# Four different orders over the token columns, one for each pair of weight ring slots

## The reference

```python
for i in range(DEPTH):                                   # DEPTH = 2
    h = layer_norm(ALPHA * h + 0.5 * swiglu_ffn(h, ffn_w_in[i, 0], ffn_w_out[i, 0]), ...)
    mix = short_conv_mixer(h, ...) if i % 2 == 0 else gla_mixer(h, ...)
    h = layer_norm(ALPHA * h + mix, ...)
    h = layer_norm(ALPHA * h + 0.5 * swiglu_ffn(h, ffn_w_in[i, 1], ffn_w_out[i, 1]), ...)
return h[:, N_META:]

def swiglu_ffn(h, w_in, w_out):
    gate, up = jnp.split(h @ w_in, 2, axis=-1)
    return (jax.nn.silu(gate) * up) @ w_out
```

## Time and profile before

| | |
|---|---|
| median of 2 runs | 1005.82 us (1005.6 to 1006.03) |
| profiled execution, its own time | 1004.9 us |
| span from its first to its last instruction | 1003.2 us |
| mean granted TensorE clock | 0.998 of full speed |
| matmuls | 7932 |
| busy: TensorE, VectorE, ScalarE, GpSimd | 990.9, 720.5, 511.1, 121.4 us |

### The profile page before, as it was taken

The page is one execution under the profiler, slowest core; times in us unless marked ns, Lnnn a source line. Parts: engine busy times, 40 slices in busy tenths (PEclk is TensorE's granted clock), DMA queues, the critical chain, the costliest instruction groups (busy, mean ns, idle before and its releaser), DMA issues.

```text
span 1003.2 us, 19130 instructions
## 1 busy us (share of the span) xinstructions
PE 990.9 (99%) x7932; PEld 975.0 (97%) x7932; DVE 720.5 (72%) x1077; ACT 511.1 (51%) x743; POOL 121.4 (12%) x136
## 2 busy tenths in 40 slices
PE   9999999999999999999999999999989999999997
PEld 7999999999999999999999999999989999999986
DVE  5866657689899865667697655667897998866543
ACT  6644345465456534344564434445867766544340
POOL 2000002320002000003220000134152320000000
PEclk9999999999999999999999999999999999999999
DMA  9976656637862865556638665565355738966531
GB/s 257 256 205 175 180 163 182 187 94 208 236 178 83 248 194 171 177 170 178 190 99 258 179 180 167 164 177 148 85 148 153 205 106 238 257 194 194 188 130 42
DMA packets 324264, 176.60 MB, mean 176 GB/s; under 512 B 6658, under 2 KB 320048, under 8 KB 324176
## 3 DMA queue, kind: packets, MB, share of 16 engines
q1 hardware_dynamic: 323664, 174.15, 60.0%
q0 software_dynamic: 480, 1.15, 0.4%
q10 hardware_dynamic: 32, 0.07, 0.0%
HBM read 174.29 MB, written 1.05 MB: 175 GB/s over the span
## 4 chain that ended last, share of the span: by engine, by line
PE 92%; DVE 4%; ACT 1%; issue 1%; POOL 1%; POOLq 0%; DVEq 0%; ACTq 0%
PE bank L1316 23%; PE bank L1321 23%; PE bank L1319 23%; PE bank L1335 3%; PE bank L1336 3%; PE bank L1337 3%; PE bank L1476 2%; PE bank L1477 2%; PE bank L1475 2%; PE bank L1360 2%; PE bank L1361 2%; PE bank L1362 2%; DVE weights_lo L824 1%; DVE rms L1224 1%; DVE gate_area L1231 0%
## 5 line engine op out<-in xcount | busy, mean ns | idle before, releaser
L465 ACT ACTIVATE weights_hi<-raw_weights 128x1024 fp32r<-128x1024 f32 x335 | 354.0, 1059 | 401.0 <-PE bank L1321 291.2
L824 DVE TENSOR_TENSOR weights_lo<-raw_weights,weights_hi 128x1024 fp32r<-128x1024 f32 x334 | 415.1, 1249 | 195.3 <-ACT weights_hi L465 194.1
L1316 PE MATMUL bank<-x_hi,weights_hi 128*128 128x272 f32 (+1 forms) x1584 | 224.1, 283 | 0.0
L1321 PE MATMUL bank<-x_lo,weights_hi 128*128 128x272 f32 (+1 forms) x1584 | 222.3, 282 | 0.0
L1319 PE MATMUL bank<-x_hi,weights_lo 128*128 128x272 f32 (+1 forms) x1584 | 222.2, 282 | 0.0
L1316 PEld LDWEIGHTS bank<-x_hi,weights_hi 128*128 128x128 f32 x1584 | 204.0, 188 | 0.7 <-ACT qT L689 0.2
L1321 PEld LDWEIGHTS bank<-x_lo,weights_hi 128*128 128x128 f32 x1584 | 203.7, 188 | 0.0
L1319 PEld LDWEIGHTS bank<-x_hi,weights_lo 128*128 128x128 f32 x1584 | 203.7, 188 | 0.0
L1321 PE MATMUL bank<-mid_lo,weights_hi 128*128 128x272 f32 x462 | 67.0, 285 | 0.0
L1316 PE MATMUL bank<-mid_hi,weights_hi 128*128 128x272 f32 x462 | 66.9, 284 | 0.0
L1319 PE MATMUL bank<-mid_hi,weights_lo 128*128 128x272 f32 x462 | 66.9, 284 | 0.0
(11 more groups left out here) (230 smaller groups left out, 1209.0 us busy)
## 6 DMA issues: line engine op xcount, KB each, us to landing
raw_weights<-in_ffn_w_in_dram SPq DMA_DIRECT2D x176, 512.0 KB, 4.7
raw_weights<-in_ffn_w_out_dram SPq DMA_DIRECT2D x70, 512.0 KB, 3.6
raw_weights<-in_conv_w_in_dram SPq DMA_DIRECT2D x24, 512.0 KB, 4.0
raw_weights<-in_gla_w_in_dram SPq DMA_DIRECT2D x24, 512.0 KB, 3.9
raw_weights<-in_ffn_w_out_dram SPq DMA_DIRECT2D x24, 384.0 KB, 3.1
raw_weights<-in_conv_w_out_dram SPq DMA_DIRECT2D x8, 512.0 KB, 4.7
raw_weights<-in_gla_w_out_dram SPq DMA_DIRECT2D x8, 512.0 KB, 4.9
x_tok<-in_x_dram SPq DMA_DIRECT2D x2, 512.0 KB, 5.0
```

Of the source, the lines that this page charges most:

```text
L465: nc.scalar.activation(w_hi[:, n % RING, :], raw[:, n % RAW, :], ACT.Copy).then_inc(hi_split, 1)
L824: nc.vector.tensor_tensor(w_lo[:, s, :], raw[:, n % RAW, :], w_hi[:, s, :].bitcast(F32), ALU.subtract).then_inc(lo_split, 1)
L1316: nc.tensor.matmul(into, block_of(w_hi, n, k - k0), walk(hi[:, k, cols]), start=first and k == k0, stop=False)
L1321: mm = nc.tensor.matmul(into, block_of(w_hi, n, k - k0), walk(lo[:, k, cols]), start=False, stop=last and k == k1 - 1)
```

## The change

`multiply` no longer has one walk for long tiles (272 columns) and one for short ones (256). It picks the walk by the pair of ring slots in which the unit lies (`n % RING // 2`, 0 to 3):

| slot pair | long tiles | short tiles |
|---|---|---|
| 0 | runs of 4, 4 passes (as before) | runs of 4, 4 passes |
| 1 | runs of 8, 2 passes | runs of 8, 2 passes |
| 2 | runs of 2, 8 passes | runs of 2, 8 passes |
| 3 | runs of 2, 4 passes | one run (as before) |

A run is a stretch of neighbouring words; with `run` words and `passes` passes the step from one run to the next within a pass is run x passes words: 16 in the first three rows, 8 in the fourth. The numbers multiplied and summed are the same.

```diff
--- before.py
+++ after.py
@@ -1302,13 +1302,17 @@
             def block_of(w, n, k):
                 return w[:, n % RING, k * P:(k + 1) * P]
 
-            def by_rows(ap):
-                return ap.rearrange("p (i j e) -> p j i e", e=4, j=4)
+            def in_runs(run, passes):
+                return lambda ap: ap.rearrange("p (i j e) -> p j i e", e=run, j=passes)
+
+            by_rows = in_runs(4, 4)
+            LONG_WALKS = (by_rows, in_runs(8, 2), in_runs(2, 8), in_runs(2, 4))
+            SHORT_WALKS = (by_rows, in_runs(8, 2), in_runs(2, 8), lambda ap: ap)
 
             def multiply(ps, n, source, cols, k0=0, k1=KU, first=True, last=True, ready=None, before_last=None, middles=()):
 
                 hi, lo = source
-                walk = by_rows if ps.shape[-1] == T else lambda ap: ap
+                walk = (LONG_WALKS if ps.shape[-1] == T else SHORT_WALKS)[n % RING // 2]
                 into = walk(ps)
                 if ready is None and before_last is None and not middles:
                     pe.wait_ge(hi_split, n + 1)
```

## The result

The median after the change is 1356.53 us (1356.5 to 1356.57, 2 runs), against 1005.82 us before. The ratio is 1.348 with a 95% interval of 1.346 to 1.351. The prediction was 1021 us, 990 to 1068: the direction was that of its likeliest case, and the size lies far outside its range. The span grew from 1003.2 to 1354.8 us, by 351.6.

What follows compares the result with a forecast made beforehand. TensorE's matmul queue was taken as the bound, count times start-to-start pace. 2.1 + 9.2 + 3.9 = +15.2 us on the profiled 1004.9 gave 1020.1, 1021 us against the median; range 990 to 1068 us.

Steps and rivals of the forecast that it cites:

- likeliest case: Whole kernel: the prediction's own forecast of 1021 us, slightly slower, range 1011 to 1033 us, chance 0.43.
- The frame: Whole kernel: time is the number of TensorE matmuls times the start-to-start pace; 4020 long and 1104 short matmuls change.
- Parts 1 and 3: Runs of 8 in 1404 long matmuls, +2.1 us; all short tiles of `multiply`, together +3.9 us, ends 0 and +8.
- Part 2: Runs of 2 in 2616 long matmuls on pairs 2 and 3: 126 ns each, +9.2 us; ends -6.5 and +47.6 us.
- the item for runs of 2 in part 3: Runs of 2 in 360 short matmuls: slower contiguous pace, +4.5 ns each, 1.6 us.
- Rival C: 2616 long and 360 short matmuls: runs of 2 leave the weight load no spare access; up to 1068 us; chance 0.22.
- R: Theory formed after the profile, not predicted: moving operand read in aligned groups of 4 words, each costing 4 columns' time.
- Rival A: Changed tiles: run length doesn't matter, stalls come from weight loads; about 1008 us, 1003 to 1011; chance 0.24 including D.
- Rivals B and D: B: 4020 long matmuls at 120.0 ns, 996 us, chance 0.11. D: hardware order fixed, 1006 us, within Rival A's 0.24.
- the one on 4 and 8 passes of runs of 2: Long tiles of pairs 3 and 2: their two walks might differ in pace; no size given.

Runs made afterwards that it cites:

- run 11: Kernel before, with runs of 4 also for first_multiply, shift matmuls and y tiles, and multiply_raw's copy rows 276 words apart, not 274: 1008.94 us against 1005.61, ratio 1.003.
- run 7: Kernel before, with the weights of blocks 0 to 6 starting 0, 4, 8 or 2 words later on slot pairs 0 to 3: 1012.55 us.
- run 9: Kernel after with all runs of 2 undone (long tiles back to runs of 4, short to one run): 1011.29 us against 1005.61, ratio 1.005.
- runs 1 to 4: Kernel after: new orders only for the read (1353.63 us), only for the bank write (1027.65), reads 2 words earlier (1124.32), runs of 6, 10 and 12 (1077.05).
- run 2: Kernel after, with the moving operand read in contiguous order and only the PSUM bank written in the four new orders: 1027.65 us.
- runs 5 and 6: Short tiles in one run, long tiles with a different step on each slot pair: all in runs of 4 (1023.68 us), all in runs of 2 (1654.33 us).
- run 8: As run 7, but in blocks 0 to 3 the weights take every second word (pairs 1 and 3) or every fourth (pair 2): 1116.4 us.
- run 3: Kernel after, most long matmuls cut to 256 columns: runs of 4 aligned, read 2 words earlier, or bank 2 words later; one run read 2 earlier: 1124.32 us.
- run 10: Most long matmuls cut to 256 columns, all pairs in runs of 4, moving operand starting 0, 4, 8 or 12 words in: 969.49 us.

## Why the prediction was wrong, step by step

**The frame held.** That the time is a count times a pace, that no wait, DMA or other engine comes in, and the counts for each slot pair: all as read. Three small readings were off and cost nothing. TensorE's longest wait before was 2.0 us, at the very start, and not 1.5. Its idle time fell by 3.9 us (12.3 to 8.4, span less busy) where "unchanged within 1 us" was forecast. And between the two stretches of y tiles in the earlier trace rows lie several shift matmuls, of which the first two, at unit 262, come right before the pace goes from 113 to 117.9 ns. That the pace depends on what went before was a guess from this; run 11 bears it out, run 7 has a case without it.

**Parts 1 and 3 but for runs of 2 held.** Runs of 8 in long tiles: +1.5 ns forecast, +2.3 measured, 3.2 us for 2.1. Short tiles in runs of 4: +0.6 us forecast, 0.0 measured, by luck: +0.9 ns on the 240 of f3, -3.8 ns on the 48 that read y. In runs of 8: 0.9 and 1.1. One run behind another walk: 0.8 and 0.9, at a median of 117 ns, by the kind of carry-over that was read from the earlier trace rows; behind runs of 8 and one run (run 9) the same tiles of f3 stayed at 113.3, so it seems to hang on which walk goes before.

**Part 2 is the step that failed**, and the item for runs of 2 in part 3 with it: 9.2 and 1.6 us were forecast, 307.3 and 37.0 came. The step took the cost of a shorter run for stalls on top of full speed, 126 ns a matmul and 140.7 at most. The runs showed a read that goes by whole 16-byte groups, so that a run of 2 pays for 4 columns: 234.0 and 247.0 ns. The high end of part 2 was "the stalls of the worst row (13.7 ns) twice over". That put a factor of two on the 13.7 ns above full speed, when nothing in the rows excluded that a factor falls on the 113.3 ns of full speed itself. No row of before has a run under 4 words, so the trace gave no bound above, and the one that I set was a guess in the form of a computation. A bound from "half as many words for each access" would have been 2 x 113.3 + 13.7 = 240.4 ns a matmul, 117.9 more than 122.5, and 1005.8 + 2616 x 0.1179 = 1314 us with the long tiles alone, 3% under the result.

**Rival C had the right place and the wrong size.** It named the 2616 long and 360 short matmuls with runs of 2 and priced them at 1068 us in all; times above that had a chance of 0.11. Its mechanism (the weight load finds no spare access) is not what runs 1 to 4 showed: the time goes with the number of groups of the moving operand alone, at 256, 260, 264 and 272 columns with the same weight load each time. No run is without a weight load, so that part is inferred. The prediction's sign for it, "If pairs 2 and 3 lie above 128, C was right", is met and yet doesn't tell C's mechanism from R's; a sign should name a number that only its mechanism gives. Rival A (the length of a run doesn't matter) is nearly right from 4 to 8 words, 2.3 ns apart, and wrong below. Rivals B and D did not happen: no new walk of the long tiles was faster than the old one in any run, and the order of reading plainly counts. Of the warnings at the prediction's end, the one on 4 and 8 passes of runs of 2 came true, 247.0 against 234.0 ns, and is small beside the doubling.

**The rule cited beside rival A.** "Advanced Engine Details and Errata" in the Trainium skill, Memory Cachelines, has lines of 16 bytes in SBUF and says "Need at least two hits on a cacheline to absorb SRAM access latency"; the prediction read this as two being enough. The 16 bytes are borne out. Two hits are not enough for this moving operand: with two the pace is 233 to 250 ns, with four 122.5, and runs of 6 and 10 lie where a full group's price for each touched group puts them. The other rule, on non-contiguous patterns in PSUM, was set aside for runs of 4 by the earlier trace rows; run 2 shows no cost for a bank written in runs of 2 either.

**What stays open.** The 7 to 24 ns over the count of groups. It depends on the step of the moving stream (runs 5 and 6, least at 16 words), on where the weights start (run 7: some 5 ns in the short tiles of f3, up to 1 ns in the long ones), hardly in the long tiles on how many groups the load reads (run 8), and in f3 on something that runs ahead (run 11). That the two reads meet each other, as I had read it, would fit run 7 but was not shown.

## What to carry to other kernels

Give the moving operand of a float32r matmul in runs whose start and length are multiples of 16 bytes; count the aligned 16-byte groups that the pattern touches, at 4 columns' time (1.67 ns) each. Count them for the weights too, and see that they stay below the columns that are streamed meanwhile: 64 groups were hidden under 272 columns, 128 were not. In the orders tried (runs of 2, 4 and 8 words, a start 8 bytes off) the PSUM side could be walked freely. Only float32r was run, and no run of 1 or 3 words. When a change goes into a shape that no row of the trace has, put the factor on the whole operation in one end of the range, and not only on its overhead.

## What the runs showed of the hardware that was not expected

- A start 8 bytes off doubles a matmul that reads runs of 4: 114.4 to 228.1 ns at 256 columns (run 3). Starts 16, 32 or 48 bytes on don't (run 10).
- The weight load goes by spacing too: taking every fourth word brings a matmul from 122.5 to some 235 ns at 272 columns and at 256 alike, every second word costs 0.5 ns at 272, and in f3, at 256, those tiles run at 119 to 120 ns for 113.5 (run 8).
- The order in which the bank is written cost nothing measurable, in runs of 2, 4 or 8 (run 2: 126.7 ns for all).
- The stream of 256 contiguous columns in f3 ran at 113.3 or 117.8 ns throughout with no change to it, 4.5 ns on 960 matmuls, after an edit ahead of it (run 11); weights that start 2, 4 or 8 words later bring it from 113.5 to 118.4 to 118.8 ns (run 7).
